# Gates' projection and ada rows placed between attention steps, with a batched compressed path

## The reference

```python
mod = silu(c) @ ada_w + ada_b                 # six rows: shift, scale, gate, twice
h = rms_norm(x, attn_pre_g) * (1 + sc_a) + sh_a
proj = h @ w_in                               # q, k/v of 3 branches, head gates, latents, merge gates
o_nsa = sum over 3 branches of g_b * softmax(q k_b) v_b   # 16 heads, 4 groups, head size 64
o_mla = softmax(q k) v                        # 16 latent heads of 96, values of 64
merged = sigmoid(g0) * (o_nsa @ w_n) + sigmoid(g1) * (o_mla @ w_m)
x = x + g_a * rms_norm(merged @ w_out, attn_post_g)
h = rms_norm(x, ffn_pre_g) * (1 + sc_f) + sh_f
x = x + g_f * rms_norm(peer_ffn(h), ffn_post_g)           # 8 heads x 16 experts a token, rows gathered
```

## Time and profile before

| | us |
|---|---|
| median of three runs | 2543.59 (2540.73 to 2543.63) |
| profiled execution: span from first to last instruction | 2542.4 |
| TensorE busy | 2051.8 (81%) |
| VectorE busy | 1338.4 (53%) |
| GpSimd busy | 764.2 (30%) |
| ScalarE busy | 438.9 (17%) |
| mean granted clock of TensorE | 0.866 |

### The profile page before, as it was taken

How to read it: one execution, slowest core, us unless ns; L and a number is a source line. 1 busy time by engine, 2 the same in 40 slices (tenths; PEclk the granted TensorE clock), 3 DMA queues, 4 the chain that set the end, 5 groups by cost and what they waited for, 6 DMA issues and landing times.

```text
span 2542.4 us, 19623 instructions
## 1 busy us (share of the span) xinstructions
PE 2051.8 (81%) x5897; PEld 1095.6 (43%) x5897; DVE 1338.4 (53%) x2241; ACT 438.9 (17%) x911; POOL 764.2 (30%) x751
## 2 busy tenths in 40 slices
PE   2697999989898778969687778787758788887786
PEld 0232443436676666769333333333323333333332
DVE  5777005701445765464565555565556555655544
ACT  0000000101333323333111111111111111111110
POOL 2111001000001320000544365444544465444551
PEclk8899999997656999989788888888879888888888
DMA  9999659942000443525799999999999999999996
GB/s 347 347 358 413 219 163 378 354 132 83 33 0 1 170 169 133 199 91 198 308 416 415 423 413 417 419 416 423 414 414 392 422 418 411 419 414 423 415 416 277
DMA packets 163863, 779.89 MB, mean 307 GB/s; under 512 B 15304, under 2 KB 23660, under 8 KB 87788
## 3 DMA queue, kind: packets, MB, share of 16 engines
q0 software_dynamic: 92800, 645.96, 62.0%
q1 hardware_dynamic: 69008, 129.65, 14.7%
q10 hardware_dynamic: 2016, 3.80, 0.4%
HBM read 777.22 MB, written 2.13 MB: 307 GB/s over the span
## 4 chain that ended last, share of the span: by engine, by line
PE 38%; DMA 29%; issue 10%; DVE 10%; POOL 9%; SPq 2%; ACT 1%; DVEq 0%; POOLq 0%; ACTq 0%
DMA arena<-in_peer_u_dram,idx_now 22%; PE PS L911 13%; PE PS L1188 10%; POOL arena L611 8%; DMA arena<-in_ada_w_dram 3%; PE PS L896 3%; DMA arena<-in_w_in_dram 3%; PE PS L898 3%; PE PS L897 3%; DVE arena L1271 1%; SPq L394 1%; PE PS L982 1%; DVE w_lo L1540 1%; PE PS L1018 1%; PE PS L1011 1%
## 5 line engine op out<-in xcount | busy, mean ns | idle before, releaser
L1188 PE MATMUL PS<-arena 128*128 128x512 f32 x2048 | 1025.2, 665 | 282.8 <-ACT arena L845 282.8
L1691 DVE CUSTOM_DVE_ANT_0 arena<-arena 128x2048 f32<-128x2048 f32 x256 | 586.5, 2293 | 490.4 <-DMA arena<-in_peer_u_dram,idx_now 489.7
L1188 PEld LDWEIGHTS PS<-arena 128*128 128x128 f32 x2048 | 433.7, 215 | 874.4 <-issue 540.0
L911 PE MATMUL PS<-arena 128*128 128x512 f32 (+1 forms) x912 | 396.1, 595 | 22.3 <-DMA arena<-in_w_in_dram 21.7
L611 POOL DMA_INDIRECT arena<-in_peer_v_dram,idx_now x256 | 317.0, 1238 | 274.5 <-PE PS L1188 205.1
L611 POOL DMA_INDIRECT arena<-in_peer_u_dram,idx_now x256 | 317.7, 1241 | 97.8 <-issue 73.1
L911 PEld LDWEIGHTS PS<-arena 128*128 128x128 f32 x912 | 175.5, 194 | 242.2 <-issue 201.8
L1540 DVE TENSOR_TENSOR w_lo<-w_raw,w_hi 128x1024 fp32r<-128x1024 f32 x96 | 134.8, 1415 | 148.8 <-ACT w_hi L764 147.8
L839 ACT ACTIVATE act_g<-dots 128x4 f32<-128x4 f32 x64 | 13.1, 205 | 946.4 <-DVE dots L1691 946.4
L602 POOL COPY idx_now<-idx_next 128x16 uint32<-128x16 uint32 x16 | 3.7, 229 | 574.2 <-DVE idx_next L1668 574.2
L1247 DVE SCALAR_TENSOR_TENSOR arena<-arena,csil 128x2048 f32<-128x2048 f32 x60 | 141.1, 2352 | 44.5 <-DMA arena<-in_ada_w_dram 44.1
(11 more groups left out here) (241 smaller groups left out, 1981.0 us busy)
## 6 DMA issues: line engine op xcount, KB each, us to landing
arena<-in_ada_w_dram POOLq DMA_DIRECT2D x96, 1024.0 KB, 9.7
arena<-in_w_in_dram SPq DMA_DIRECT2D x112, 512.0 KB, 10.5
w_raw<-in_w_out_dram SPq DMA_DIRECT2D x32, 512.0 KB, 3.4
w_raw<-in_peer_w_q_dram SPq DMA_DIRECT2D x32, 512.0 KB, 3.5
w_raw<-in_w_branch_nsa_dram SPq DMA_DIRECT2D x16, 512.0 KB, 3.6
w_raw<-in_w_branch_mla_dram SPq DMA_DIRECT2D x16, 512.0 KB, 3.5
arena<-in_cmp_w_dram SPq DMA_DIRECT2D x8, 512.0 KB, 3.9
arena<-in_peer_u_dram,idx_now POOLq DMA_INDIRECT x256, 16.0
```

Of the source, the lines that this page charges most:

```text
L911: ins = nc.tensor.matmul(PS[:, (n % 2) * 2 + t, 0:cols], lhs[:, kk, t * P:(t + 1) * P], wring[:, (m + w) % WSLOTS, k, 0:cols], start=(kk = ...
L1188: ins = nc.tensor.matmul(PS[:, bank + k, :], diag[e % 8], Vrow[e % RING][:, k * NC:(k + 1) * NC], start=False, stop=False, skip_group_chec ...
L1691: v.tensor_tensor_reduce(row, row, h2[:, t, :], 1.0, 0.0, ALU.mult, ALU.add, dots[:, e:e + 1]).then_inc(u_free, 1)
```

## The change

The buffers are laid out anew in on-chip memory. The order of work becomes:

- The chunks of `w_in` come in the order `MAIN`: keys and values first. The rotation and the duplication of keys, the compression products, and the transposes of all keys and all queries (`kT`, `qT`, 16 transposes each) stand between the chunks. Scores, softmax and transposes of the compressed branch are done once for all 16 heads.
- Chunk 0 of the merge gates stays behind the tail. Chunks 1 to 4 are cut into 8 tiles each, and each of the 32 sparse steps has one (`gate_products`: four products after `score`, four recorded ones before and four after `turn`). Chunk 5 stands alone behind the up projections. Chunks 6 and 7 lie in the 16 latent steps. The gates leave PSUM unchanged; the sigmoid comes later, in ScalarE's loop beside `w_high`.
- Of the 64 ada rows 16 are added before attention, and one in each of the 48 steps, on VectorE between `mask_max` and `normalise`. From row 18 on, only two slots of the ring are used. The column sums stand at steps 0 and 16, after the sparse steps and after the latent ones.
- `normalise` divides the probabilities before `turn` (two `tensor_scalar`). `weigh` multiplies values (stationary, 64 columns) with the turned probabilities (256 and 128 columns); the outputs of the branches and of a pair of heads add up in one PSUM bank, transposed already, and ScalarE (`pair_out`) and VectorE (`pair_low`) split them straight into `oT_hi`, `oT_lo`. POOL's staging, `o_nsa`, `o_mla` and their transposes go.
- Since `oT_hi` takes their place, the three full rows are made only after `merged_ready`, at the start of the out product, and `X` is loaded again there (two loads of 1 MB from ScalarE's queue). VectorE waits for the first row (`rows_ready`) before its first `w_low` of the out product, as before.
- At the end of each token tile's experts, ScalarE squares the PSUM banks in four instructions in place of one copy to `yacc`, and VectorE's squaring goes.

```diff
+        X0 = at(o_g + 16 * KW, NT, D)
+        ada_ring = at(o_e, ADA_SLOTS, D)
...
+        qT = at(o_e + 16 * KW, PAIRS, SEQ)
+        kT = at(o_e + 24 * KW, 2, GROUPS, SEQ)
+        qm = at(o_e + 16 * KW, NT, HEADS * MD)
...
+        oT_hi, oT_lo = split_at("oT_hi", o_f, 16, SEQ), split_at("oT_lo", o_f + 16 * KW, 16, SEQ)
...
+        MAIN = (2, 3, 4, 0, 1, 5)
+        def gate_tile(c_):
+            return W_TAIL + 8 + 8 * c_ if c_ < 5 else W_G5 + 8 * (c_ - 5)
...
+        def ada_slot(r):
+            if r < KD:
+                return r % 4, 16 * (2 * KD // 4 + r // 4 + 1)
+            return r % 2, 16 * (2 * KD // 4 + KD // 4 + (r - KD) // 2 + 1)
...
+            load_chunk(W_C4, MAIN[4] * NC)
+            load_chunk(W_C5, MAIN[5] * NC)
+            load_chunk(W_TAIL, TAIL0, TAIL)
+            for c_ in range(5):
+                load_chunk(gate_tile(c_), GM0 + c_ * NC)
...
+            for c_ in range(5, CH_GATE):
+                load_chunk(gate_tile(c_), GM0 + c_ * NC)
...
+            def ada_row(r):
+                seg, j = 2 + r // KD, r % KD
+                pool.wait_ge(ada_used, ROW0 - 3 + r if r < KD + 2 else ROW0 - 1 + r)
+                pool.dma_start(ada_ring[:, ada_slot(r)[0], :], ada_v[:, j, seg * D:(seg + 1) * D]).then_inc(
+                    ada_in[ada_slot(r)[0]], 16)
...
+            for r in range(8, 4 * KD):
+                ada_row(r)
+            pool.wait_ge(mod_stored, 16 * 4)
+            pool.wait_ge(merged_ready, 1)
...
+            def gate_chunk_out(c_):
+                act.wait_ge(w_used, gate_tile(c_) + 8)
+                for t in range(NT):
+                    ins = nc.scalar.copy(gates_v[:, t, c_ * NC:(c_ + 1) * NC], PS[:, 6 + t, :])
+                ins.then_inc(gate_out, 1)
+            def mod_out(k):
+                act.wait_ge(ada_cols, 2 * QTRS + k + 1)
+                if k:
+                    act.wait_ge(mod_stored, 16 * k)
+                nc.scalar.copy(mod_sb, PS[:, 5, :]).then_inc(mod_ready, 1)
+                act.wait_ge(mod_ready, k + 1)
+                act.dma_start(mod_dram[k, :].rearrange("(k n) -> k n", k=4), mod_sb[0:P:32, :]).then_inc(mod_stored, 16)
...
+            def probs_out(n):
+                act.wait_ge(pt_in, n + 1)
+                if n >= 2:
+                    act.wait_ge(weighed, n - 1)
+                nc.scalar.copy(probT[:, n % 2, :], PS[:, 2 + n % 2, 0:384]).then_inc(pt_out, 1)
+            def pair_out(p):
+                act.wait_ge(weighed, 4 * (p + 1) if p < PAIRS else NSA_UNITS + 2 * (p - PAIRS + 1))
+                nc.scalar.copy(oT_hi[:, p, :], PS[:, 4, 0:SEQ]).then_inc(o_hi, 1)
+            for n in range(NSA_UNITS + 3):
+                if n % 16 == 0 and n < NSA_UNITS:
+                    mod_out(n // 16)
+                if n and n % 8 == 0:
+                    gate_chunk_out(n // 8)
+                if n < NSA_UNITS:
+                    softmax_exp(n, NSA_SCALE)
+                if n >= 6 and (n - 6) % 4 == 0:
+                    pair_out((n - 6) // 4)
+                if 1 <= n <= NSA_UNITS:
+                    probs_out(n - 1)
+            mod_out(2)
...
+                    if m in (4, 5, 6, 7):
+                        t, b = m % 2, m // 2 % 2
+                        part = gates[:, t, b, bass.ds(i * NC, NC)]
+                        nc.scalar.activation(part, part, ACT.Sigmoid).then_inc(gate_sig, 1)
+            act.wait_ge(merged_ready, 1)
+            for t in range(NT):
+                act.dma_start(X[:, t, :], x_v[:, t, :]).then_inc(x2_in, 16)
...
+            def gate_products(c_, w, k):
+                m = gate_tile(c_) + w
+                if k == 0:
+                    tile_ready(m)
+                ins = products(6, m, w, k, hT, KD)
+                if k == 1:
+                    ins.then_inc(w_used, 1)
...
+            def weigh(n, head, v, first, last):
+                dst = PS[HD * (head % 2):HD * (head % 2) + HD, 4, :]
+                pe.wait_ge(pt_out, n + 1)
+                nc.tensor.matmul(dst[:, 0:SEQ], v(0), probT[:, n % 2, 0:SEQ], start=first, stop=False)
+                ins = nc.tensor.matmul(dst[:, P:SEQ], v(1), probT[:, n % 2, SEQ:SEQ + P], start=False, stop=last)
+                ins.then_inc(weighed, 1)
+                return ins
...
+            for n in range(NSA_UNITS + 2):
+                if n % 16 == 0 and n < NSA_UNITS:
+                    column_sums(n // 16)
+                if n < NSA_UNITS:
+                    h, b = n // 2, n % 2
+                    half = slice(HD * (h % 2), HD * (h % 2) + HD)
+                    score(n, lambda t: qT[half, h // 2, t * P:(t + 1) * P], lambda lo, hi: kT[half, b, h // RPG, lo:hi])
+                    if n >= 8 and n % 8 == 0:
+                        pe.wait_ge(gate_out, n // 8)
+                    gate_products(1 + n // 8, n % 8, 0)
+                if 1 <= n <= NSA_UNITS:
+                    turn(n - 1)
+                if n < NSA_UNITS:
+                    gate_products(1 + n // 8, n % 8, 1)
+                if n >= 2:
+                    h, b = (n - 2) // 2, (n - 2) % 2
+                    g, r = h // RPG, h % RPG
+                    if b == 0:
+                        if h % 2 == 0 and h:
+                            pe.wait_ge(o_lo, h // 2)
+                        nc.tensor.matmul(PS[HD * (h % 2):HD * (h % 2) + HD, 4, 0:SEQ], vc[32 * r:32 * r + 32, g, :],
+                                         PcT[32 * r:32 * r + 32, g, :], start=True, stop=False)
+                    v0 = KV0 + ((b + 1) * 2 + 1) * GROUPS * HD + g * HD
+                    weigh(n - 2, h, lambda kt: proj[:, kt, v0:v0 + HD], False, b == 1)
+            column_sums(2)
...
+            for w in range(8):
+                for k in range(2):
+                    gate_products(5, w, k)
...
+            for n in range(HEADS + 2):
+                if n < HEADS:
+                    pe.wait_ge(mt_out, n + 1)
+                    score(NSA_UNITS + n, lambda t: mT[0:MD, n % 2, t, :],
+                          lambda lo, hi: mT[0:MD, n % 2, 2:4, :].rearrange("p a b -> p (a b)")[:, lo:hi])
+                    if n == 8:
+                        pe.wait_ge(gate_out, 6)
+                    gate_products(6 + n // 8, n % 8, 0)
+                if n + 1 < HEADS:
+                    turn_heads(n + 1)
+                if 1 <= n <= HEADS:
+                    turn(NSA_UNITS + n - 1)
+                if n < HEADS:
+                    gate_products(6 + n // 8, n % 8, 1)
+                if n >= 2:
+                    h = n - 2
+                    if h % 2 == 0:
+                        pe.wait_ge(o_lo, PAIRS + h // 2)
+                    weigh(NSA_UNITS + h, h, lambda kt: kvm[:, kt, h * 2 * MN + MN:(h + 1) * 2 * MN], True, True)
+            column_sums(3)
...
+            def ada_row(r):
+                seg, j = 2 + r // KD, r % KD
+                slot, landed = ada_slot(r)
+                dve.wait_ge(ada_in[slot], landed)
+                w = ada_ring[:, slot, :]
+                if j:
+                    dve.wait_ge(ada_used, ROW0 + r)
+                    ins = v.scalar_tensor_tensor(out=acc, in0=w, scalar=csil[:, j:j + 1], in1=acc,
+                                                 op0=ALU.mult, op1=ALU.add)
+                else:
+                    dve.wait_ge(ada_cols, 2 * QTRS + seg - 2)
+                    ins = v.tensor_scalar(acc, w, csil[:, 0:1], None, ALU.mult)
+                ins.then_inc(ada_used, 1)
...
+            def normalise(n, gate=None):
+                r = n % 2
+                dve.wait_ge(exp_done, n + 1)
+                link(v.reciprocal(srec[:, r, :], ssum[:, r, :]))
...
+                v.tensor_scalar(s_prob[:, r, 0:P], s_prob[:, r, 0:P], srec[:, r, 0:1], None, ALU.mult)
+                v.tensor_scalar(s_prob[:, r, P:3 * P], s_prob[:, r, P:3 * P], srec[:, r, 1:2], None, ALU.mult).then_inc(
+                    prob_ready, 1)
+            def pair_low(p):
+                dve.wait_ge(o_hi, p + 1)
+                v.tensor_tensor(oT_lo[:, p, :], PS[:, 4, 0:SEQ], oT_hi[:, p, :].bitcast(F32), ALU.subtract).then_inc(o_lo, 1)
+            for n in range(NSA_UNITS + 3):
+                if n < NSA_UNITS:
+                    mask_max(n, NSA_SCALE)
+                    ada_row(KD + n)
+                    normalise(n, gnsa[:, :, 3 * (n // 2) + n % 2 + 1])
+                if n >= 6 and (n - 6) % 4 == 0:
+                    pair_low((n - 6) // 4)
...
```

More of the change, by code:

```diff
@@ L402, in _ @@
-            with sp.Fori(0, CH_MAIN - CH_FIRST) as i:
-                for k in range(8):
-                    load(CH_FIRST * 8 + k, win_v[:, 2 * k:2 * k + 2, bass.ds(i * NC + CH_FIRST * NC, NC)], i=i, step=8)
+                load(m, win_v[:, 4 * q + 2 * h:4 * q + 2 * h + 2, MAIN[c_] * NC:(MAIN[c_] + 1) * NC])
+            load_chunk(W_C2, MAIN[2] * NC)
+            load_chunk(W_C3, MAIN[3] * NC)
             for k in range(8):
-                load(W_TAIL + k, win_v[:, 2 * k:2 * k + 2, CH_MAIN * NC:GM0], cols=TAIL)
@@ L407, in _ @@
[L407 to L413 removed]
```

(76 more changed lines are left out.)

1032 lines of the change are left out of this document (437 added, 595 removed).

## The result

The changed kernel takes 2430.86 us (median of 4 runs, 2428.13 to 2433.83), the kernel before 2543.61 us beside it (2540.73 to 2544.23): ratio 0.956, 95% interval 0.954 to 0.957. The forecast was 2444. The profiled run took 2433.43 us, span 2431.7.

What follows compares the result with a forecast made beforehand. Bound: attention's TensorE work at half clock and waits between its steps. -103 to the first branch product, -20 branch products, +24 out product, -0.5 experts' ends: -99.4 on 2542.4, 2443; median 1.2 above, 2444; 8-in-10 range 2392 to 2492.

Steps and rivals of the forecast that it cites:

- The mechanism: Attention: TensorE's work, at clock 0.51 in sparse attention before, runs near 1.0 with eight gates' instructions in each step.
- Up to the first sparse step: From the first stage's end at 168.9 us: 205 us of projections, products and waits, so attention starts at 374 instead of 648.5.
- the 32 small score products: Compressed branch, before the first sparse step: priced at 4 us on TensorE.
- The steps: Sparse attention: TensorE sets each step at 5.4 us; with waits, shape changes, column sums and ends 203 us, to 577.
- A change of shape: Attention steps on TensorE: 0.1 us each (bounds none and 0.3), 112 sparse and 32 latent changes, 14 us.
- the dear rival: Attention steps: a change of shape costs 0.3 us, 144 changes add 29 us, total 2473; chance 0.12.
- Pairs' waits: Attention steps: TensorE waits for `pair_low` every other head, 7 times 1.2 us in sparse and 7 times 0.6 in latent.
- The ada ring: Rival, attention steps: landings of 11.0 us with two slots make 7.0 us a step, +43, 2487; chance 0.14.
- Column sums: Ada rows' sums on TensorE around the attention steps: priced at 3.5 us each.
- Branch products: Behind attention: the three rows' preparation leaves, so about 20 of 23.5 us of TensorE's waits for `w_low` go.
- Out product: Behind the merge: TensorE stalls 11 us for the first row and POOL's operations collide for 13, together +24.
- The rest: The experts' ends: a copy and a square of 2 us swapped for four squares, -0.5 us.

Runs made afterwards that it cites:

- experiment 1: Changed kernel with six chunks of gates' products as whole blocks ahead of the sparse and latent steps instead of in them: 2576.33 us, ratio 1.016.
- experiment 4: Kernel before, with four unread products of 128 x 512 columns ahead of each unit's score in both attentions: 2648.13 us, ratio 1.044.
- experiment 2: Changed kernel with gates' products as whole blocks, and VectorE's row operations in the 48 steps on 512 of 2048 columns: 2547.76 us, ratio 1.004.
- experiment 3: Changed kernel with VectorE's row operations in the 48 steps on only 512 of 2048 columns: 2422.83 us, ratio 0.955.
- experiment 5: Changed kernel with the copies of a finished pair of heads ahead of the step's exponentials and maxima: 2422.3 us, ratio 0.956.
- Experiment 10: Changed kernel with VectorE's wait for the first modulation row moved behind the out product's first eight low parts: 2413.25 us, ratio 0.951.
- experiment 7: Changed kernel with the first modulation row prepared during the branch products, in its own place, instead of after the merge: 2422.13 us, ratio 0.956.

## Why the prediction was right, step by step

**The mechanism** held. The clock in the steps is 1.00, and experiments 1 and 4 show both directions: without the gates' products it falls to 0.51 in the sparse steps, and idle products in the old kernel lift it to 0.95. The Trainium skill (TensorE: Matmul & The Clock Gate, HAM oscillation) lays the fall to pauses for data between bursts. The traces here agree with it only in part. Experiments 1 and 2, whose sparse steps have waits and stand at 0.51, fit it. But the sparse steps of the changed kernel had seven waits of up to 0.7 us for a pair and kept 1.00. And TensorE ran at half the clock with no pause at all: in the compression products of the kernel before, busy for 25.25 of 26.0 us at 0.52, and in the small score products of the changed kernel, here TensorE's timeline and the window:

```profile
332.55 12.97 PE L964 MATMUL PS<-kcT,arena 64*128 64x15 f32 x64 [4.16 <-DVE arena L1394]
```
```profile
332.50:345.60 13.10, 13.05 (x65) 13.05 (x65) 0.04 (x1) 1.02 (x1) 0.00 (x0) 0.50 0.01 1
```

Each stands behind a wait, of 3.2 us and 4.2 us, with which the clock may have fallen; that it stayed low through 13 and 26 us of narrow products without a gap is not explained by pauses. Which property of the work holds the clock up stays open.

**Up to the first sparse step**, forecast 205 us behind the first stage: measured 213.7 to the column sum (the stage itself ended 3.4 us earlier). The waits for the queries' copies, 4.2 us, came as forecast (4.4). The term that was off is the 32 small score products of the compressed branch: I had them at 4 us, they took 13.0 at clock 0.50, and the chunk behind them 30.5 instead of 27.7. The compression products took 24.6 us against my 22, since their weights come late (3.2 us in the two longest waits). Transposes, value products and copies, cheaper than forecast, give some of it back.

**The steps.** 203 us forecast for the sparse ones, 197.2 measured. A change of shape costs 0.1 us at the full clock as well: from start to start L1002's pair takes 0.32 behind a change, against 0.23 in the earlier trace rows, and L1003's 0.53 ahead of one, against 0.43. The rule of the Trainium skill (TensorEngine Tiling (Array Packing), Key Properties) that a changed mode drains TensorE fits a cost at each change; the price is a third of what the dear rival needed. Pairs' waits were 6.2 us in all where I had 12.6; experiments 3 and 5 put them at 6.6. The ada ring never set the step: its loads landed in 5.5 us in the median, not 9.7.

**Column sums** had the wrong price: 3.5 us each by the row of the old form, whose four products all write partition 0, against 1.07 for the new one, which writes four groups of 32 partitions. Four times 2.43 make 9.7 of the 14.8 us by which the first branch product came earlier than forecast. The first stage gives 3.4, the pairs' waits 6.4, the stretch ahead of the steps takes 8.7; the other 4.0 are spread over the steps and the ends, and I did not follow them.

**Branch products**: -20 forecast, -20.9 measured. **Out product**: +24 forecast as a stall of 11 and collisions of 13, +30.8 measured. Experiment 10 splits it: without the wait the stretch is 13.4 us over the kernel before, which I lay to the collisions; the wait is 17.5, of which 5.2 its own, the rest later loads and a lower clock. I had the place right and the size of the stall by luck. The row was ready 24 us behind the merge, where I had 25, but TensorE had 20 us of work until then (839.05 to 859.05), not 15. A gap of some 11 us is in the trace as I had named it, yet it is a later load's; this follower was missing from the forecast. **The rest**: -0.5 forecast, -3.1 measured.

So -14.8 before the branch products, -0.9 in them, +6.8 behind the merge and -2.6 at the end make -11.5 us, against -11.3 between the forecast span of 2443 and the measured 2431.7; the rest is rounding. The forecast was good in its sum also because errors of up to 10 us in single terms cancelled: the small score products against the column sums, for one.

Slips in the prediction's working, each within 1 us: the two chunks of the earlier trace rows are 55.20 us, not 55.1; a pair's wait is 5.6 - 4.5 = 1.1 us, not 1.2; 25 less 15 is a stall of 10, not 11; and the four terms of the sum add up to -99.5, not -99.4.

## What to carry to other kernels

Work of TensorE that must be done anyway is cheap in a stage whose clock stands at half without it: move it there in pieces, and count both its price and the halved price of what stands beside it. How cheap depends on what else fills the stage: beside the ada rows on VectorE 115 us of gates' products made the sparse steps 17.7 us longer (experiment 1), while in the old kernel 173 us of added products cost 110 (experiment 4). A wait belongs directly ahead of the instruction that needs it: with a ring behind it, a stall of 5.2 us made a stretch 17.5 us longer. Products with few columns of weights go into different groups of columns.

## What the runs showed of the hardware

Four float32 products with 32 columns of weights and 512 columns, into four groups of 32 partitions, took 1.07 us together; into one group 3.62 us. Products of 128 x 512 that nobody reads raised the granted clock of the sparse stage from 0.51 to 0.95, and 173 us of them in both attentions cost 110. Products with 15 and 60 columns, one behind the other without a gap, ran at 0.50 and 0.52. A low part of 128 x 1024 on VectorE took 1.23 us, and 3.6 to 4.8 us beside GpSimd's operations on 128 x 2048 (experiments 7 and 10).
